# Fourier mixing over tokens split by mirror symmetry, in a two-layer diffusion block

## Chip and metric

The kernel runs on one core of a Trainium2 chip. The metric is the device time of one execution in microseconds, the median of several runs. The core has TensorE (PE in the rows, with PEld for its weight loads), VectorE (DVE), ScalarE (ACT), GpSimd (POOL) and SyncE (SP), which here issues most DMAs. DVE, ACT and POOL work on vectors; PE alone writes the accumulators in PSUM, in 8 banks of 512 fp32 columns.

## The reference

Two layers work on 512 latent tokens and 256 context tokens of 1024 channels; the last layer (layer 1) only on the latent ones. Each layer has a token mixer of three branches (attention, Fourier mixing, an RWKV scan), gated and merged, and then a convolutional feed-forward part. The Fourier branch takes 512 channels in 4 groups of 128 and transforms over channels of a group and over tokens, keeping the real part:

```python
def _fourier(pf):
    B, T, _ = pf.shape
    z = jnp.fft.fftn(pf.astype(jnp.float32).reshape(B, T, F_GROUPS, F_GROUP_W), axes=(1, 3), norm='ortho')
    return z.real.reshape(B, T, D_F).astype(pf.dtype)
...
    y = g[..., 0, :] * (o_a @ lp['w_pa']) + g[..., 1, :] * (o_f @ lp['w_pf']) + g[..., 2, :] * (o_c @ lp['w_pc'])
    return y @ lp['w_o']
```

## The kernel before

The kernel is written engine by engine, with semaphores. The function `close` is the last stage of a layer's token mixer; it runs once in layer 0 (768 tokens) and once in layer 1 (512). Its PE program is a list of 24 slots: 8 slots `pc` (one output tile of 128 channels each, product of the RWKV result with `w_pc`), 8 slots `pf` (Fourier result with `w_pf`), 8 slots `o` (output projection). A `pc` or `pf` slot has four contraction tiles k, and for each three products (high part by high weight, low part by high weight, high part by low weight), since every operand is split into two fp32r parts whose sum is nearly fp32. So a slot is 12 products, each of 512 and, in layer 0, 256 columns; `fm_product` (L370) issues them.

For each slot n, ACT applies the sigmoid to the slot's gate, then splits the weights of slot n + 2 (`split`, L2023: `w_hi`; it waits for the end of slot n, since the ring holds two), POOL computes `w_lo`, DVE multiplies the slot's result by the gate (L2124) and adds it to `y` (L2129). SP loads weights and gates ahead, in program order.

The Fourier transform is put between the products of the `pc` slots, one step after the second k (h = 0) and one after the fourth (h = 1) of a slot. For group j, a `z` step multiplies two token tiles of the input `f` by a 128 x 256 table of cosines and sines over channels (`dft_w`, L1938), and DVE copies the result into `z`, a double buffer (L2072). When all of a group's `z` is there, the `of` step sums over tokens with the full cosine and sine tables `dft_lat` (512 x 512 each, L1947) and `dft_ctx` (256 x 256 each, L1951). ACT rounds the result out of PSUM to `of_hi` (L2038), DVE takes the rest as `of_lo` (L2075). The first `pf` slot (slot 8) waits for `of_lo` of group k before its k-th contraction tile. All these transform matmuls are plain fp32. A list sets the order:

```python
dft = [s for j in range(F_GROUPS) for s in [("z", j, i) for i in range(HT2)] + [("of", j, 0)]]
dft_at = {(n, h): dft[2 * n + h] for n in range(KT) for h in range(2) if 2 * n + h < len(dft)}
```

The buffers `f` and `z` lie in the space of `x`, which is read back from memory behind the weights of slot 11.

Of the kernel before, what the change touches and what calls it, by code (L numbers as in the profile page):

```python
# [22 lines left out]
F32 = mybir.dt.float32  # L23
# [6 lines left out]
P = 128  # L30
# [40 lines left out]
def tables():  # L71
# [63 lines left out]
def program(nc, A, out):  # L135
    with ExitStack() as top:
# [1701 lines left out]
        def close(l, oc, y, rings, last):  # L1838
# [7 lines left out]
            dft = [s for j in range(F_GROUPS) for s in [("z", j, i) for i in range(HT2)] + [("of", j, 0)]]  # L1846
            dft_at = {(n, h): dft[2 * n + h] for n in range(KT) for h in range(2) if 2 * n + h < len(dft)}
# [8 lines left out]
            with ExitStack() as s2, stage(nc) as (block, sem):  # L1856
# [657 lines left out]
```

## Time and profile before

| | |
|---|---|
| median of 3 runs | 3658.41 us (3656.13 to 3660.78) |
| profiled execution, span from first to last instruction | 3653.4 us |
| median of the runs less that span | 5.0 us |
| PE busy | 3375.0 us, 92% of the span |
| DVE, ACT, POOL busy | 1582.8, 1268.5, 1071.4 us |
| closing stage of layer 0, slots 0 to 8 | about 1277.5 to 1362.9 us |
| closing stage of layer 1, slots 0 to 8 | about 3112.8 to 3179.4 us |

The profiled execution's own time beside its span isn't recorded; the runs' median lies 5.0 us above the span. Busy time is an average over stages; what a change is worth is read in the stage that it touches.

### The profile page before, as it was taken

To read this page: it belongs to the slowest core of one execution; us is meant where nothing else is said; L and a number is where in the kernel's file an instruction comes from. 1 tells how busy PE (TensorE), PEld (TensorE's weight loads), DVE (VectorE), ACT (ScalarE), POOL (GpSimd) and SP (SyncE) were. 2 spreads that over 40 slices of the span, in tenths; PEclk is the share of its full clock that TensorE was granted. 3 is DMA by queue.
4 is the path that set the end of the run, shared out by engine and by line. 5 is a ranking of instruction groups with operands and counts; after the bars stand their busy time and mean duration, and the time that the engine had idled before them with its cause. 6 is when DMAs were issued, how large, how long until landed. Compare 5 with 4: busy or idle time off the path is not lost. (4 is left out here: it accounts for less than half of the span.)

```text
span 3653.4 us, 82760 instructions
## 1 busy us (share of the span) xinstructions
PE 3375.0 (92%) x36725; PEld 2696.8 (74%) x36725; DVE 1582.8 (43%) x2538; ACT 1268.5 (35%) x2184; POOL 1071.4 (29%) x645
## 2 busy tenths in 40 slices
PE   6989999999888999799999899999899898889998
PEld 4668888888655777687878676887778666568887
DVE  3243334442377546512112734445453476372224
ACT  3333233333365412321212243334344465233222
POOL 1111133233011412332333132223333114235553
PEclk8999999999999999999999999999999999989999
DMA  7664333443212343233332145344343313423332
GB/s 260 213 204 113 111 113 90 119 121 96 83 58 96 102 140 104 81 116 121 116 116 94 50 142 182 101 113 128 115 128 92 104 58 121 165 84 104 98 98 87
DMA packets 444861, 423.43 MB, mean 116 GB/s; under 512 B 15652, under 2 KB 372042, under 8 KB 437594
## 3 DMA queue, kind: packets, MB, share of 16 engines
q1 hardware_dynamic: 442922, 409.35, 35.7%
q10 hardware_dynamic: 1584, 8.78, 0.6%
q8 instruction: 291, 4.77, 0.5%
q14 instruction: 64, 0.52, 0.0%
HBM read 329.34 MB, written 88.74 MB: 114 GB/s over the span
## 5 line engine op out<-in xcount | busy, mean ns | idle before, releaser
L893 PE MATMUL ps<-I-321_h_hi,I-324_w_hi 128*128 128x256 f32 (+1 forms) x832 | 294.8, 354 | 4.5 <-PEq L124 4.5
L893 PE MATMUL ps<-I-322_h_lo,I-324_w_hi 128*128 128x256 f32 (+1 forms) x832 | 282.0, 339 | 0.0
L893 PE MATMUL ps<-I-321_h_hi,I-325_w_lo 128*128 128x256 f32 (+1 forms) x832 | 281.8, 339 | 0.0
L2372 POOL TENSOR_TENSOR I-18800_w_lo<-I-18798_w_raw,I-18799_w_hi 128x1024 fp32r<-128x1024 f32 x60 | 145.1, 2418 | 342.6 <-ACT I-18799_w_hi L2335 342.5
L893 PE MATMUL ps<-I-23550_h_hi,I-23553_w_hi 128*128 128x512 f32 (+1 forms) x544 | 212.7, 391 | 4.6 <-PEq L124 4.6
L893 PE MATMUL ps<-I-23551_h_lo,I-23553_w_hi 128*128 128x512 f32 (+1 forms) x544 | 200.9, 369 | 0.0
L893 PE MATMUL ps<-I-23550_h_hi,I-23554_w_lo 128*128 128x512 f32 (+1 forms) x544 | 200.6, 369 | 0.0
L2372 POOL TENSOR_TENSOR I-39040_w_lo<-I-39038_w_raw,I-39039_w_hi 128x1024 fp32r<-128x1024 f32 x60 | 144.5, 2408 | 154.6 <-ACT I-39039_w_hi L2335 154.6
L2335 ACT ACTIVATE I-18799_w_hi<-I-18798_w_raw 128x1024 fp32r<-128x1024 f32 x61 | 64.6, 1059 | 355.0 <-PE ps L370 235.3
L370 PE MATMUL ps<-I-18795_h_hi,I-18799_w_hi 128*128 128x512 f32 x704 | 182.8, 341 | 1.1 <-DVE I-18796_h_lo L407 1.1
L370 PE MATMUL ps<-I-18795_h_hi,I-18800_w_lo 128*128 128x512 f32 x704 | 182.6, 340 | 0.0
L370 PE MATMUL ps<-I-18796_h_lo,I-18799_w_hi 128*128 128x512 f32 x704 | 180.1, 337 | 0.0
L893 PEld LDWEIGHTS ps<-I-321_h_hi,I-324_w_hi 128*128 128x128 f32 x832 | 158.5, 191 | 25.4 <-issue 4.9
L857 POOL TENSOR_TENSOR I-325_w_lo<-I-323_w_raw,I-324_w_hi 128x1024 fp32r<-128x1024 f32 x34 | 81.9, 2408 | 320.1 <-ACT I-324_w_hi L1137 320.1
L893 PEld LDWEIGHTS ps<-I-321_h_hi,I-325_w_lo 128*128 128x128 f32 x832 | 158.5, 191 | 17.2
L893 PEld LDWEIGHTS ps<-I-322_h_lo,I-324_w_hi 128*128 128x128 f32 x832 | 158.8, 191 | 14.6
L1119 ACT ACTIVATE I-1999_result<-ps 128x512 f32<-128x512 f32 x104 | 51.3, 493 | 327.7 <-PE ps L893 327.5
L857 POOL TENSOR_TENSOR I-23554_w_lo<-I-23552_w_raw,I-23553_w_hi 128x1024 fp32r<-128x1024 f32 x34 | 83.7, 2462 | 275.7 <-ACT I-23553_w_hi L1137 275.7
L963 PE MATMUL ps<-I-49_x 64*64 64x32 f32 x3840 | 149.3, 220 | 1.4 <-issue 1.4
L370 PE MATMUL ps<-I-39035_h_hi,I-39039_w_hi 128*128 128x512 f32 x352 | 137.9, 392 | 1.1 <-DVE I-39036_h_lo L407 1.1
L370 PE MATMUL ps<-I-39036_h_lo,I-39039_w_hi 128*128 128x512 f32 x352 | 137.1, 389 | 0.0
L370 PE MATMUL ps<-I-39035_h_hi,I-39040_w_lo 128*128 128x512 f32 x352 | 137.0, 389 | 0.0
(902 smaller groups left out, 8757.7 us busy)
## 6 DMA issues: line engine op xcount, KB each, us to landing
I-323_w_raw<-in_w_in SPq DMA_DIRECT2D x67, 512.0 KB, 5.8
I-23552_w_raw<-in_w_in SPq DMA_DIRECT2D x67, 512.0 KB, 5.2
I-18808_ada_w<-in_ada_w SPq DMA_DIRECT2D x24, 1024.0 KB, 6.0
I-18798_w_raw<-in_ffn_up SPq DMA_DIRECT2D x44, 512.0 KB, 3.8
I-39038_w_raw<-in_ffn_up SPq DMA_DIRECT2D x44, 512.0 KB, 3.8
proj_d<-I-1999_result SPq DMA_DIRECT2D x52, 384.0 KB, 3.0
I-507_ada_w<-in_ada_w SPq DMA_DIRECT2D x16, 1024.0 KB, 5.8
I-18798_w_raw<-in_ffn_down SPq DMA_DIRECT2D x22, 512.0 KB, 3.3
```

Of the source, the lines that this page charges most:

```text
L370: m = pe.matmul(dst[:, at:at + n], w[wi][:, k, :], a[ai][:, k, at:at + n], start=k == 0 and i == 0, stop=k == kt - 1 and i == 2)
L857: pool.tensor_tensor(lo(s), raw(s), hi(s).bitcast(F32), ALU.subtract).then_inc(sem("w_lo"), 1)
L893: m = pe.matmul(bank(6 + i % 2, n_c), w[:, k, :], hv[:, k, c0:c0 + n_c], start=k == 0 and v == 0, stop=k == KT - 1 and v == 2)
L963: return pe.matmul(side(ps[rows(i), (2 + d) * 512 + c0:(2 + d) * 512 + c0 + C], n_lv, 1 - d), Y[d][rows(i), c0:c0 + C], side(TT[d][rows(i) ...
L1119: act.activation(res[:, s % 2, c0:c0 + n_c], bank(6 + i % 2, n_c), ACT.Copy, scale=DH_A ** -0.5 if J_Q <= slots[s][0] < J_K else 1.0).then ...
L2335: act.activation(pair(g)[0], rings[0][:, g % 3, :, :], ACT.Copy).then_inc(sem("w_hi"), 1)
L2372: pool.tensor_tensor(pair(g)[1], rings[0][:, g % 3, :, :], pair(g)[0].bitcast(F32), ALU.subtract).then_inc(sem("w_lo"), 1)
```

## The change

The token transform is folded. For tokens t and n - t, cosine tables are equal and sine tables opposite, so the input's mirrored tokens are summed (DVE) and subtracted (POOL) once, for all groups: blocks E0, E1 (sums), O0, O1 (differences), E0M (a second form of the first block, which odd outputs need), and CE, CO, CEM for the context. A `z` step now multiplies 128-token blocks by the cosine or the sine table alone (128 columns each): 8 blocks a group in layer 0, 5 in layer 1, in two steps. The `of` step computes half of the outputs: even-numbered cosine outputs, odd-numbered cosine outputs (both written to every second column of PSUM) and sine outputs, from tables with half the rows. ACT copies the sine half out of PSUM (`odd`), DVE forms output m as cosine less sine and output n - m as cosine plus sine, in descending order, and copies outputs 0 and n/2; ACT then rounds to `of_hi` and DVE takes `of_lo`, both now from SBUF. The steps stand at other places: the first `z` after slot 1, the last `of` in the middle of slot 7, and each `of_hi`/`of_lo` half a slot after its sums.

```diff
-        both = np.stack([np.cos(at) * s, -np.sin(at) * s])
+        half = n // 2
+        folded = np.concatenate([np.cos(at)[:half, 0:half + 1:2], np.cos(at)[:half, 1:half:2], np.sin(at)[:half, 1:half]], 1) * s
...
-            dft = [s for j in range(F_GROUPS) for s in [("z", j, i) for i in range(HT2)] + [("of", j, 0)]]
-            dft_at = {(n, h): dft[2 * n + h] for n in range(KT) for h in range(2) if 2 * n + h < len(dft)}
+            dft = [("z", 0, 0), ("z", 0, 1)]
+            for j in range(F_GROUPS):
+                dft += [("z", j + 1, 0), ("of", j, 0), ("z", j + 1, 1)] if j + 1 < F_GROUPS else [("of", j, 0)]
+            dft_at = {((i + 3) // 2, (i + 3) % 2): s for i, s in enumerate(dft)}
+            rest_at = {((i + 4) // 2, (i + 4) % 2): j for i, (kind, j, _) in enumerate(dft) if kind == "of"}
+            E0, E1, O0, O1, E0M, CE, CO, CEM = range(8)
+            z_blocks = ((E0, E1, O0, O1), (E0M,) if last else (E0M, CE, CO, CEM))
...
-                    sp.dma_start(dw[:, :], A["dft_w"]).then_inc(sem("f"), 16)
                     gate_in(0)
                     weights(2)
-                    sp.dma_start(dl[:, :, :, :], A["dft_lat"]).then_inc(sem("dft"), 16)
-                    sp.dma_start(dc[:, :, :, :], A["dft_ctx"]).then_inc(sem("dft"), 16)
+                    sp.dma_start(dw[:, :], A["dft_w"]).then_inc(sem("dft"), 16)
+                    sp.dma_start(dl[:, :, :], A["dft_lat"]).then_inc(sem("dft"), 16)
+                    sp.dma_start(dc[:, :, :], A["dft_ctx"]).then_inc(sem("dft"), 16)
...
                             if c == 0:
-                                pe.wait_ge(sem("f"), 32)
+                                pe.wait_ge(sem("dft"), 48)
+                                pe.wait_ge(sem("fold_e"), len(f_seqs))
+                                pe.wait_ge(sem("fold_o"), len(f_seqs))
                             if c >= 2:
                                 pe.wait_ge(sem("z"), c - 1)
-                            for t in (2 * i, 2 * i + 1):
-                                m = pe.matmul(bank(4 + c % 2, 2 * P, (t % 2) * 2 * P), f[:, j, t * P:(t + 1) * P], dw[:, :], start=True, stop=True)
+                            for q, b in enumerate(z_blocks[i]):
+                                w = dw[:, P:2 * P] if b in (O0, O1, CO) else dw[:, 0:P]
+                                m = pe.matmul(bank(4 + i, P, q * P), fold[:, j, b, :], w, start=True, stop=True)
...
-                            pe.wait_ge(sem("z"), HT2 * (j + 1))
+                            pe.wait_ge(sem("z"), 2 * j + 2)
                             if j:
-                                pe.wait_ge(sem("of_lo"), j)
-                            for i in range(2 * LT):
-                                m = pe.matmul(bank(6), z[:, j % 2, i % LT, (i // LT) * P:(i // LT + 1) * P], dl[:, i // LT, i % LT, :],
-                                              start=i == 0, stop=i == 2 * LT - 1)
...
+                                pe.wait_ge(sem("of_sum"), j)
+                            for (_, n, e, o, em, at), table in zip(f_seqs, (dl, dc)):
+                                half, last_k = n // 2, n // (2 * P) - 1
+                                cos_e, cos_o, sin = slice(0, half // 2 + 1), slice(half // 2 + 1, half + 1), slice(half + 1, n)
+                                for k in range(last_k + 1):
+                                    pe.matmul(ps[:, at:at + half + 1:2], z[:, j % 2, e + k, :], table[:, k, cos_e], start=k == 0, stop=k == last_k)
+                                for k in range(last_k + 1):
+                                    pe.matmul(ps[:, at + 1:at + half + 1:2], z[:, j % 2, e + k if k else em, :], table[:, k, cos_o],
+                                              start=k == 0, stop=k == last_k)
+                                for k in range(last_k + 1):
+                                    m = pe.matmul(ps[:, at + half + 1:at + n], z[:, j % 2, o + k, :], table[:, k, sin], start=k == 0, stop=k == last_k)
...
                                 act.wait_ge(sem("ofmm"), j + 1)
-                                act.activation(ofp[0][:, j, :], of_ps, ACT.Copy).then_inc(sem("of_hi"), 1)
+                                if j >= 2:
+                                    act.wait_ge(sem("of_sum"), j - 1)
+                                for o, w, _, _, _, at in f_seqs:
+                                    m = act.activation(odd[:, j % 2, o // 2:o // 2 + w // 2 - 1], ps[:, at + w // 2 + 1:at + w], ACT.Copy)
+                                m.then_inc(sem("odd"), 1)
+                            if (n, h) in rest_at:
+                                j = rest_at[n, h]
+                                act.wait_ge(sem("of_sum"), j + 1)
+                                act.activation(ofp[0][:, j, :], of[:, j % 2, 0:n_tok], ACT.Copy).then_inc(sem("of_hi"), 1)
...
+                        pool.tensor_tensor(blocks_of(o, half // P)[:, :, 1:half], f[:, :, at + 1:at + half],
+                                           f[:, :, at + w - 1:at + half:-1], ALU.subtract).then_inc(sem("fold_o"), 1)
...
+                        for dst, n in ((blocks_of(e, half // P), half), (blocks_of(em, 1), P)):
+                            dve.tensor_tensor(dst[:, :, 1:n], f[:, :, at + 1:at + n], f[:, :, at + w - 1:at + w - n:-1], ALU.add)
...
+                                dve.tensor_tensor(v[:, 1:half], even[:, 1:half], sines, ALU.subtract)
+                                dve.tensor_tensor(v[:, w - 1:half:-1], even[:, 1:half], sines, ALU.add)
+                                m = dve.tensor_copy(v[:, 0:half + 1:half], even[:, 0:half + 1:half])
+                            m.then_inc(sem("of_sum"), 1)
...
+                    def of_rest(j):
+                        dve.wait_ge(sem("of_hi"), j + 1)
+                        dve.tensor_tensor(ofp[1][:, j, :], of[:, j % 2, 0:n_tok], ofp[0][:, j, :].bitcast(F32), ALU.subtract).then_inc(sem("of_lo"), 1)
```

The order on each engine follows from these lists, so it is shown at two places. First PE, layer 0, an `of` step among the products of a `pc` slot, in the kernel before (`ps` is PSUM, `I-49_x` the space of `x` in which `z` lies):

```order
L370 MATMUL ps<-I-17273_oc_hi,I-13892_w_lo 128x512
L370 MATMUL ps<-I-17273_oc_hi,I-13892_w_lo 128x256
L1947 MATMUL ps<-I-17276_dft_lat,I-49_x 128x512 x8
L1951 MATMUL ps<-I-17277_dft_ctx,I-49_x 128x256 x4
L370 MATMUL ps<-I-17273_oc_hi,I-13891_w_hi 128x512
```

The `of` step of group 0 after the change, in the middle of slot 3 of layer 0, on the same engine:

```order
L371 MATMUL ps<-I-17273_oc_hi,I-13892_w_lo 128x512
L371 MATMUL ps<-I-17273_oc_hi,I-13892_w_lo 128x256
L1961 MATMUL ps<-I-17276_dft_lat,I-49_x 128x129 x2
L1963 MATMUL ps<-I-17276_dft_lat,I-49_x 128x128 x2
L1966 MATMUL ps<-I-17276_dft_lat,I-49_x 128x255 x2
L1961 MATMUL ps<-I-17277_dft_ctx,I-49_x 128x65
L1963 MATMUL ps<-I-17277_dft_ctx,I-49_x 128x64
L1966 MATMUL ps<-I-17277_dft_ctx,I-49_x 128x127
L371 MATMUL ps<-I-17273_oc_hi,I-13891_w_hi 128x512
```

Twelve matmuls of 512 or 256 columns became nine of 64 to 255 columns. The second place is DVE in slots 6 and 7 of layer 0; before, from the copy of `z` in slot 6 to the last `of_lo`:

```order
L2072 COPY I-49_x<-ps 128x512
L2124 TENSOR_TENSOR I-17263_gated<-I-17262_gate,ps 128x768
L2129 TENSOR_TENSOR I-13889_y<-I-13889_y,I-17263_gated 128x768
L2072 COPY I-49_x<-ps 128x512 x2
L2124 TENSOR_TENSOR I-17263_gated<-I-17262_gate,ps 128x768
L2129 TENSOR_TENSOR I-13889_y<-I-13889_y,I-17263_gated 128x768
L2075 TENSOR_TENSOR I-17272_of_lo<-ps,I-17271_of_hi 128x768
```

On the same engine after the change, from the sums of group 2 in slot 6 to the first of group 3 in slot 7 (`I-49_x` now also holds `odd` and the sums):

```order
L2117 TENSOR_TENSOR I-49_x<-ps,I-49_x 128x255
L2118 TENSOR_TENSOR I-49_x<-ps,I-49_x 128x255
L2119 COPY I-49_x<-ps 128x2
L2117 TENSOR_TENSOR I-49_x<-ps,I-49_x 128x127
L2118 TENSOR_TENSOR I-49_x<-ps,I-49_x 128x127
L2119 COPY I-49_x<-ps 128x2
L2178 TENSOR_TENSOR I-17263_gated<-I-17262_gate,ps 128x768
L2183 TENSOR_TENSOR I-13889_y<-I-13889_y,I-17263_gated 128x768
L2124 TENSOR_TENSOR I-17272_of_lo<-I-49_x,I-17271_of_hi 128x768
L2109 COPY I-49_x<-ps 128x512
L2117 TENSOR_TENSOR I-49_x<-ps,I-49_x 128x255
```

The six sums came in ahead of the slot's gate product, and the copy of `z` that the `of` step of group 3 needs stands behind them and behind `of_lo`.

## Rows read from the trace of the kernel before

**Rows 1.** The page: span, then busy us, share and instructions of each engine.
```profile
span 3653.4 us, 82760 instructions
PE 3375.0 (92%) x36725; PEld 2696.8 (74%) x36725; DVE 1582.8 (43%) x2538; ACT 1268.5 (35%) x2184; POOL 1071.4 (29%) x645
```
**Rows 2.** Windows, layer 0: length, busy us of five engines (count), clock, DMA share, GB/s.
```profile
1320.00:1340.00 20.00, 20.00 (x89) 14.54 (x88) 8.60 (x8) 3.95 (x6) 2.56 (x2) 1.00 0.22 66
```
**Rows 3.** Timeline, DVE: start, length, line, output and inputs, [idle before, releaser].
```profile
1320.71 0.96 DVE L2075 TENSOR_TENSOR I-17272_of_lo<-ps,I-17271_of_hi 128x768 fp32r<-128x768 f32 x1 [6.59 <-ACT I-17271_of_hi L2038]
...
1340.30 0.96 DVE L2075 TENSOR_TENSOR I-17272_of_lo<-ps,I-17271_of_hi 128x768 fp32r<-128x768 f32 x1 [6.59 <-ACT I-17271_of_hi L2038]
...
3134.58 0.69 DVE L2075 TENSOR_TENSOR I-37914_of_lo<-ps,I-37913_of_hi 128x512 fp32r<-128x512 f32 x1 [10.86 <-ACT I-37913_of_hi L2038]
...
3160.51 0.69 DVE L2075 TENSOR_TENSOR I-37914_of_lo<-ps,I-37913_of_hi 128x512 fp32r<-128x512 f32 x1 [9.83 <-ACT I-37913_of_hi L2038]
```
**Rows 4.** Timeline, PE, an `of` step of layer 0.
```profile
1291.50 7.03 PE L1947 MATMUL ps<-I-17276_dft_lat,I-49_x 128*128 128x512 f32 x16
...
1298.37 1.89 PE L1951 MATMUL ps<-I-17277_dft_ctx,I-49_x 128*128 128x256 f32 x8
```
**Rows 5.** Timeline, PE, layer 0: the first and the last of 22 products.
```profile
1370.25 0.51 PE L370 MATMUL ps<-I-17271_of_hi,I-13892_w_lo 128*128 128x512 f32 x2
...
1377.61 0.51 PE L370 MATMUL ps<-I-17271_of_hi,I-13892_w_lo 128*128 128x512 f32 x2
```
**Rows 6.** Timeline, PE, attention of layer 0: 128-column fp32 products and their successors.
```profile
984.74 1.60 PE L1462 MATMUL ps<-I-13901_v_tm,I-13906_a_T 128*128 128x128 f32 x12
986.18 0.98 PE L1451 MATMUL ps<-I-50_ident,I-13902_E 128*128 128x128 f32 x6
```
**Rows 7.** Line 963 (the scan): passes' ns min/median/max, first and last start, shapes.
```profile
L963 PE MATMUL ps<-I-49_x x3840: 186/219/291, 296.4 to 2831.4; 64*64 64x32 f32 x192
```
**Rows 8.** Groups by line, ACT, both closing stages: count, busy us, mean ns, idle before.
```profile
L2023 ACT ACTIVATE I-13891_w_hi<-I-13890_w_raw 128x512 fp32r<-128x512 f32 x14 | 8.8, 628 | 37.7 <-PE ps L370 30.9 <-DMA I-13890_w_raw<-in_w_pf 5.8 <-DMA I-13890_w_raw<-in_w_pc 1.0
...
L2038 ACT ACTIVATE I-17271_of_hi<-ps 128x768 fp32r<-128x768 f32 x4 | 3.2, 812 | 30.0 <-PE ps L1951 30.0
...
L2038 ACT ACTIVATE I-37913_of_hi<-ps 128x512 fp32r<-128x512 f32 x4 | 2.4, 589 | 12.9 <-PE ps L1947 12.9
```
**Rows 9.** Groups by line, DVE, closing stage of layer 0.
```profile
L2124 DVE TENSOR_TENSOR I-17263_gated<-I-17262_gate,ps 128x768 f32<-128x768 f32 x15 | 14.3, 955 | 25.3 <-PE ps L370 18.8 <-issue 4.2 <-ACT I-17262_gate L2031 2.2
L2072 DVE COPY I-49_x<-ps 128x512 f32<-128x512 f32 x12 | 8.2, 687 | 8.5 <-PE ps L1938 8.5
```
**Rows 10.** Timeline, PE: two waits in later slots of both closing stages.
```profile
1380.83 0.61 PE L370 MATMUL ps<-I-17271_of_hi,I-13891_w_hi 128*128 128x512 f32 x2 [2.70 <-POOL I-13892_w_lo L2060]
...
3184.51 1.98 PE L2004 MATMUL ps<-I-37906_part,I-51_ones 128*128 128x512 f32 x4 [2.33 <-DVE I-37906_part L2139]
```
**Rows 11.** Windows after those two waits (the clock is the third figure from the end).
```profile
1381.00:1385.00 4.00, 4.00 (x15) 3.38 (x16) 3.97 (x7) 1.79 (x3) 1.28 (x1) 0.57 0.71 197
3185.00:3191.00 6.00, 6.00 (x25) 4.36 (x24) 3.00 (x6) 2.23 (x4) 0.00 (x0) 1.00 0.97 412
```
**Rows 12.** Timeline, PE: the waits at the start of both closing stages.
```profile
1282.50 1.13 PE L1938 MATMUL ps<-I-17275_dft_w,I-49_x 128*128 128x256 f32 x4 [0.80 <-DMA I-17275_dft_w<-in_dft_w]
...
3112.83 0.79 PE L370 MATMUL ps<-I-37915_oc_hi,I-35365_w_hi 128*128 128x512 f32 x1 [4.13 <-DVE I-37916_oc_lo L2116]
...
3117.03 2.08 PE L1938 MATMUL ps<-I-37917_dft_w,I-49_x 128*128 128x256 f32 x4 [1.27 <-DMA I-37917_dft_w<-in_dft_w]
...
3124.80 7.13 PE L1947 MATMUL ps<-I-37918_dft_lat,I-49_x 128*128 128x512 f32 x16 [0.56 <-DMA I-37919_dft_ctx<-in_dft_ctx]
```
**Rows 13.** Groups by line, POOL, closing stage of layer 0.
```profile
L2060 POOL TENSOR_TENSOR I-13892_w_lo<-I-13890_w_raw,I-13891_w_hi 128x512 fp32r<-128x512 f32 x14 | 18.1, 1292 | 101.8 <-ACT I-13891_w_hi L2023 101.8
```
**Rows 14.** Timeline, DVE, layer 1: gate products of slots 6 and 7.
```profile
3173.72 0.69 DVE L2124 TENSOR_TENSOR I-37905_gated<-I-37904_gate,ps 128x512 f32<-128x512 f32 x1 [1.46 <-PE ps L370]
...
3176.52 0.69 DVE L2124 TENSOR_TENSOR I-37905_gated<-I-37904_gate,ps 128x512 f32<-128x512 f32 x1 [1.38 <-PE ps L370]
```

More of the change, by code:

```diff
@@ L1949, in transform @@
-                            if not last:
-                                for i in range(2 * CT):
-                                    m = pe.matmul(bank(7, 256), z[:, j % 2, LT + i % CT, (i // CT) * P:(i // CT + 1) * P], dc[:, i // CT, i % CT, :],
-                                                  start=i == 0, stop=i == 2 * CT - 1)
+                                pe.wait_ge(sem("of_sum"), j)
[9 more added lines that the diff above has]
+                                    m = pe.matmul(ps[:, at + half + 1:at + n], z[:, j % 2, o + k, :], table[:, k, sin], start=k == 0, stop=k == last_k)
@@ L2057, in _ @@
                 def _(pool):
+                    for at, w, _, o, _, _ in f_seqs:
+                        pool.memset(blocks_of(o, w // (2 * P))[:, :, 0:1], 0.0)
+                    pool.wait_ge(sem("f"), 16)
+                    for at, w, _, o, _, _ in f_seqs:
+                        half = w // 2
+                        pool.tensor_tensor(blocks_of(o, half // P)[:, :, 1:half], f[:, :, at + 1:at + half],
+                                           f[:, :, at + w - 1:at + half:-1], ALU.subtract).then_inc(sem("fold_o"), 1)
                     for n in range(2, N):
@@ L2071, in transformed @@
                                 dve.wait_ge(sem("ofmm"), j - 1)
[L2072 removed]
+                            dve.tensor_copy(z[:, j % 2, 4 * i:4 * i + n, :].rearrange("p a b -> p (a b)"), bank(4 + i, n * P)).then_inc(sem("z"), 1)
                         else:
[L2074 to L2075 removed]
+                            dve.wait_ge(sem("odd"), j + 1)
+                            if j >= 2:
+                                dve.wait_ge(sem("of_lo"), j - 1)
+                            for o, w, _, _, _, at in f_seqs:
+                                half, v = w // 2, of[:, j % 2, o:o + w]
+                                even, sines = ps[:, at:at + half + 1], odd[:, j % 2, o // 2:o // 2 + half - 1]
+                                dve.tensor_tensor(v[:, 1:half], even[:, 1:half], sines, ALU.subtract)
[5 more added lines that the diff above has]
+                        dve.tensor_tensor(ofp[1][:, j, :], of[:, j % 2, 0:n_tok], ofp[0][:, j, :].bitcast(F32), ALU.subtract).then_inc(sem("of_lo"), 1)
                     def y_rest(j):
@@ L2116, in _ @@
                         dve.tensor_tensor(ocp[1][:, k, :], oc[:, k, 0:n_tok], ocp[0][:, k, :].bitcast(F32), ALU.subtract).then_inc(sem("oc_lo"), 1)
+                    dve.wait_ge(sem("f"), 16)
+                    for at, w, e, _, em, _ in f_seqs:
+                        folds(at, w, e, em)
                     for n in range(M):
+                        if (n, 0) in rest_at:
+                            of_rest(rest_at[n, 0])
                         if (n, 0) in dft_at:
@@ L2129, in _ @@
                         dve.tensor_tensor(yj, yj, pr[:, n % 2, 0:n_tok], ALU.add).then_inc(sem("ysum"), 1)
+                        if (n, 1) in rest_at:
+                            of_rest(rest_at[n, 1])
                         if (n, 1) in dft_at:
```

28 lines of the change are left out of this document (16 added, 12 removed).

## The prediction

> **What bounds the kernel now.** I read the page first: TensorE is busy for 92% of the span and no other engine for half of it [rows 1], so a change to TensorE's work counts at full size wherever TensorE runs without gaps. Next, the windows over the two closing stages, the only ones that the change touches: in layer 0, from 1320 to 1340 us, PE is busy in all 20 us at the full 2.4 GHz [rows 2]. Then the timeline there, engine by engine. DVE's `of_lo` of two neighbouring groups starts 19.57 us apart in layer 0; in layer 1 two groups take 25.93 us [rows 3]. DVE and ACT wait for PE in between. The stage is bound by PE alone, and its rhythm tells what the transform costs.
>
> **PE, removed.** Each fp32 matmul shows as two passes. The `of` step of layer 0 starts 16 latent passes at 1291.50 and the first context pass at 1298.37: 0.429 us for 512 columns, so 0.215 for 256 [rows 4]. A group is three `z` steps of 4 passes (2.58), 16 latent passes (6.87) and 8 context passes (1.72): 11.17 us. The rhythm agrees: 21 products after 1370.25 the clock stands at 1377.61, 0.350 us each [rows 5], so two slots of 12 take 8.40, and 19.57 less that is 11.17. In layer 1 a group is 1.72 and 6.87, 8.59 us; half of 25.93 less one and a half slots of 2.80, the distance of two slots without transform [rows 14], leaves 8.77, a little of it waiting.
>
> **PE, added.** The nearest row for 128 columns on fresh weights is the attention's fp32 product: 12 passes start at 984.74 and what follows them at 986.18, 0.120 a pass [rows 6]. Per group, layer 0: `z` is 8 blocks, 16 passes, 1.92; the latent part 8 passes of 128 or 129 columns at 0.120 and 4 of 255 at 0.214, 1.82; the context part 6 short passes, which I also take at 0.120, 0.72; together 4.46. Layer 1: 10 passes (1.20) and 1.82, 3.02. Saved: 4 x (11.17 - 4.46) = 26.8 and 4 x (8.59 - 3.02) = 22.3, **49.1 us**. If short passes cost only their columns (0.107 for 128), 3.3 us more is saved.
>
> Two thirds of the latent passes now write every second PSUM column, which the trace does not show. Bounds: the small products of the scan write runs with holes between them, and all 3840 of their passes lie between 186 and 291 ns, the median 219 [rows 7], which speaks for no cost; the bound above is that the latent ones take twice their columns' time, 0.214 in place of 0.120: 8 x 0.094 x 8 groups = 6.0 us. I take nothing, being nearest to rows 7, and keep 6.0 for the range.
> The Trainium skill speaks against the change here: its page "SBUF — State Buffer", section "Door 1: The DMA port swizzle", says that PSUM has lines of two fp32 values and that any non-contiguous access there slows matmuls significantly. No row of before writes single columns with gaps; by that rule, read as a doubling, the time would be the rival's below, by rows 7 it is the forecast's.
>
> **The waits that take part of it back.** Before, a result went PE, ACT (`of_hi`), DVE (`of_lo`), while PE had `z` steps of the next group ahead. Now it is a chain through four instructions, ACT (`odd`), DVE (sums), ACT (`of_hi`), DVE (`of_lo`), and three of its places in the program put it behind other work. In slots 3, 6 and 7 ACT must first split the weights of slot n + 2, and that waits for the END of slot n; `odd` stands behind it though its matmuls end mid-slot. DVE waits for `odd`, and behind that wait are the slot's gate product and addition, the `of_lo` and the copy of `z` that PE's next `of` needs. Prices: split 0.63 [rows 8]; `odd` 255 + 127 columns: the PSUM copy is 0.81 for 768 and 0.59 for 512 [rows 8], so 0.37 + 0.26, and 0.37 in layer 1; sums: DVE takes 0.955 for a product of 768 and 0.687 for a copy of 512 [rows 9], 1.05 ns a column on 0.15, so 2 x 0.42 + 2 x 0.28 + two tiny copies 0.3 = 1.65 (pipelined), and 1.0 in layer 1; gate product, addition, `of_lo` at a spacing of 0.90 and 0.62; the copy 0.68, or 0.28 for a single block; 0.1 for each change of engine.
>
> - From the end of slot 6, layer 0: 0.1 + 0.63 + 0.63 + 0.1 + 1.65 + 3 x 0.90 + 0.68 + 0.1 = 6.6 us until the `z` of group 3 is whole. PE has a `z` step (0.96) and half a slot (2.10) before `of` of group 3: a stall of 3.5. Layer 1: 4.5 against 0.24 + 1.40: 2.9.
> - From the end of slot 7: the same without the copy, 5.8, until `of_lo` of group 3; slot 8 needs it at its fourth k, 3.15 later: 2.6. Layer 1: 4.1 against 2.1: 2.0.
> - From the end of slot 3, group 0: 6.6 against 0.96 + 4.20 + 0.96: 0.5; layer 1: 4.5 against 0.24 + 2.80 + 0.96: 0.5.
> - In slot 5 DVE's `of_lo` of group 1 waits for ACT, again behind a split: 0.1 + 0.63 + 0.81 + 0.1 + 0.95 + 0.68 + 0.1 = 3.4 from the end of the slot, against 0.96 + 2.10: 0.4; layer 1 about the same, 0.4.
>
> Layer 0 loses 7.0, layer 1 5.8: **12.8 us**. If reversed operands take DVE twice as long, for which no row speaks (L2117 writes ascending, L2118 descending), each sum grows by 0.70 and 0.42, over 4 groups in each layer 4.5 us more.
>
> The clock: after a gap of 2.70 us before 1380.83 the granted clock was 0.57 of full on average from 1381 to 1385, half clock for most of them, which lost 4 x 0.43 = 1.7 us; after a gap of 2.33 before 3184.51 it stayed at 1.00 [rows 10, 11]. Of the stalls above two are longer than 2.70 and two are at or below it: 2 x 1.7 = **3.4 us**, with 0 and 6.8 as ends.
>
> **The start.** Layer 1 starts at 3112.83, waits 1.27 for `dft_w` and 0.56 for `dft_ctx`, and reaches its first `of` at 3124.80 [rows 12]: 11.97 us for 18 products and 2 `z` steps, which cost 5.9 at full clock: 6.1 lost, 1.8 of it in those waits, the rest to the clock after a wait of 4.13. Now 24 products run first without a wait, and I take half of the loss as gone; the tables shrink from 2.5 MB to 0.63, all landing before PE asks. Against that stand the folds: DVE 1020 and 508 columns (1.2 + 0.7 + two tiny, 2.2 us; 3.9 with the context), and POOL 1020 (+ 508) at 1292 ns for 512 [rows 13], 2.6 (+ 1.3), while each delays the other. They begin when `f` lands, just before 1282.50 and 3117.03, where `dft_w` behind it in the queue ends a wait [rows 12]. In layer 1 they end near 3120, where PE gets there; in layer 0 between 1286 and 1289.5, PE arriving near 1288. DVE's first gate product stands behind the folds, but slot 2 alone asks for it; POOL's split for slot 2 likewise. I take 3 us gained in layer 1 and 1 lost in layer 0, **2 us** gained, ends -2 and +4.
>
> **Nothing else moves.** Slots without transform ran 2.80 us apart in layer 1 (3173.72 to 3176.52) [rows 14], 12 products of 0.233, so loading weights and gates hides behind products alone. `x` returns on SP behind the gate of slot 11, which waits for slot 8's gate product, later than `of_lo`; the stall that it brings after [rows 10] stays.
>
> **The sum.** 49.1 + 2 - 12.8 - 3.4 = 34.9 us. The profiled execution spans 3653.4 us, so 3618.5 after; the median of the runs lies 5.0 above that span, and I keep that distance: **3623.5 us**.
>
> **Rivals.**
> - Strided PSUM writes slow the matmuls: + 6 us and up, 3630 to 3640. For it: no row writes single columns. Against it: rows 7. Chance 0.14.
> - The waits don't bind, since ACT or DVE runs ahead of my walk: 12.8 and 3.4 come back, 3607. Against it: `odd` stands behind the split in every one of the three slots. Chance 0.10.
> - More waiting than walked (clock falls in four places, folds late, reversed operands twice as long): 3.4 + 4 + 4.5 more, 3635 to 3640. Chance 0.10.
> - Slower than before: reversed operands run element by element on DVE. A sum's reversed half is 0.70 us in layer 0 and 0.42 in layer 1, and each of the 8 sums lies on a chain without slack; 34.9/(4 x 1.12) = 7.8, so from some nine times the plain duration on the time exceeds 3658. No row of DVE speaks for such a factor. Chance 0.05.
> - My forecast, all of it within 3613 to 3634: 0.61.
>
> The range 3610 to 3639 leaves out most of the second rival, the slow one and the edges. A measurement of this kernel tells 0.2% (7 us) from no change: faster 0.93, same 0.02, slower 0.05.
>
> **What would show it.** Right: `z` passes near 0.12 us apart; PE idle near 3 us in slot 7 before the `of` of group 3, released by DVE's copy, and near 2.5 us in slot 8, released by `of_lo`; `odd` on ACT always after a split; time from the first product of the stage to the end of slot 8 shorter by about 16 to 20 us in each layer. Wrong: cosine passes of 128 columns spaced over 0.2 us, sums over 2 us on DVE, or PE waiting for the folds by more than 2 us.

## The result and the profile after

The changed kernel takes 3616.11 us in the median of four runs (3612.46 to 3627.61) against 3657.27 before: a ratio of 0.9896, 95% interval 0.9881 to 0.9911. Its profiled execution took 3612.46 us and spans 3610.6, 42.8 less than the span in [rows 1]. The page (busy us, share and instructions of each engine):

```profile
span 3610.6 us, 82796 instructions
PE 3321.2 (92%) x36709; PEld 2677.0 (74%) x36709; DVE 1601.1 (44%) x2582; ACT 1271.8 (35%) x2196; POOL 1081.1 (30%) x651
```

PE lost 54 us of work, DVE and POOL gained 18 and 10. To see where the time went I cut the span at the first product of each closing stage and at DVE's gate product of slot 8, which ends the part that the change touches:

| us | start to layer 0 | stage, layer 0 | between | stage, layer 1 | to the end |
|---|---|---|---|---|---|
| before | 1277.49 | 85.73 | 1749.61 | 66.60 | 473.97 |
| after | 1274.55 | 66.50 | 1749.05 | 46.36 | 474.14 |

The two stages became 19.2 and 20.2 us shorter, 39.5 together (forecast 34.9); the other 3.3 lie where nothing was changed. The timeline of PE in layer 0 shows the price of the transform, and what it gives back (start, busy us, tile, passes, [idle before, releaser]):

```profile
1274.55 1.01 PE L371 MATMUL ps<-I-17273_oc_hi,I-13891_w_hi 128*128 128x512 f32 x2 [4.62 <-DVE I-17274_oc_lo L2165]
...
1288.05 1.13 PE L1951 MATMUL ps<-I-17275_dft_w,I-17278_folded 128*128 128x128 f32 x8 [2.24 <-issue]
...
1291.12 1.06 PE L1951 MATMUL ps<-I-17275_dft_w,I-17278_folded 128*128 128x128 f32 x8
...
1294.12 1.05 PE L1951 MATMUL ps<-I-17275_dft_w,I-17278_folded 128*128 128x128 f32 x8
...
1297.12 0.61 PE L1961 MATMUL ps<-I-17276_dft_lat,I-49_x 128*128 128x129 f32 x4
1297.57 0.61 PE L1963 MATMUL ps<-I-17276_dft_lat,I-49_x 128*128 128x128 f32 x4
1298.01 1.03 PE L1966 MATMUL ps<-I-17276_dft_lat,I-49_x 128*128 128x255 f32 x4
...
1301.63 1.06 PE L1951 MATMUL ps<-I-17275_dft_w,I-17278_folded 128*128 128x128 f32 x8
...
1319.01 0.71 PE L1961 MATMUL ps<-I-17276_dft_lat,I-49_x 128*128 128x129 f32 x4 [0.58 <-DVE I-49_x L2109]
...
1329.66 0.71 PE L1961 MATMUL ps<-I-17276_dft_lat,I-49_x 128*128 128x129 f32 x4 [2.85 <-DVE I-49_x L2109]
...
1339.71 0.62 PE L371 MATMUL ps<-I-17271_of_hi,I-13891_w_hi 128*128 128x512 f32 x2 [2.09 <-DVE I-17272_of_lo L2124]
```

Two `z` steps start 3.00 us apart with six products (2.10) between them: 0.90 for 8 passes, 0.112 a pass. Four strided cosine passes take 0.45 and 0.44, the same 0.112; an `of` step is 4.51 - 2.10 = 2.41. A group costs 2 x 0.90 + 2.41 = 4.21 us (11.17 before). In layer 1 a slot's half is six products of 0.233, 1.40:

```profile
3103.22 1.05 PE L1951 MATMUL ps<-I-37963_dft_w,I-37966_folded 128*128 128x128 f32 x8
...
3105.50 0.61 PE L1961 MATMUL ps<-I-37964_dft_lat,I-49_x 128*128 128x129 f32 x4
...
3108.64 0.38 PE L1951 MATMUL ps<-I-37963_dft_w,I-37966_folded 128*128 128x128 f32 x2
...
3110.26 1.06 PE L1951 MATMUL ps<-I-37963_dft_w,I-37966_folded 128*128 128x128 f32 x8
```

The distances 2.28, 3.14 and 1.62 less 1.40 are `z` steps of 0.88 and 0.22 and an `of` of 1.74, which make 2.84 a group (8.59 before). There PE stands three times for long enough to be listed:

```profile
3120.77 0.71 PE L1961 MATMUL ps<-I-37964_dft_lat,I-49_x 128*128 128x129 f32 x4 [0.63 <-DVE I-49_x L2109]
...
3128.22 0.71 PE L1961 MATMUL ps<-I-37964_dft_lat,I-49_x 128*128 128x129 f32 x4 [2.40 <-DVE I-49_x L2109]
...
3135.46 0.50 PE L371 MATMUL ps<-I-37959_of_hi,I-35411_w_hi 128*128 128x512 f32 x1 [1.73 <-DVE I-37960_of_lo L2124]
```

Why PE waits before 1329.66 is read on ACT and DVE, from the end of slot 6 (1323.9) on. ACT first:

```profile
1323.91 0.63 ACT L2037 ACTIVATE I-13891_w_hi<-I-13890_w_raw 128x512 fp32r<-128x512 f32 x1 [6.27 <-PE ps L371]
1324.44 0.54 ACT L2055 ACTIVATE I-49_x<-ps 128x255 f32<-128x255 f32 x2
1326.32 0.84 ACT L2060 ACTIVATE I-17271_of_hi<-I-49_x 128x768 fp32r<-128x768 f32 x1 [1.34 <-DVE I-49_x L2119]
```

and DVE:

```profile
1325.01 0.42 DVE L2117 TENSOR_TENSOR I-49_x<-ps,I-49_x 128x255 f32<-128x255 f32 x1 [3.60 <-ACT I-49_x L2055]
1325.35 0.41 DVE L2118 TENSOR_TENSOR I-49_x<-ps,I-49_x 128x255 f32<-128x255 f32 x1
...
1326.20 0.94 DVE L2178 TENSOR_TENSOR I-17263_gated<-I-17262_gate,ps 128x768 f32<-128x768 f32 x1
1327.18 0.96 DVE L2183 TENSOR_TENSOR I-13889_y<-I-13889_y,I-17263_gated 128x768 f32<-128x768 f32 x1
1328.06 0.95 DVE L2124 TENSOR_TENSOR I-17272_of_lo<-I-49_x,I-17271_of_hi 128x768 fp32r<-128x768 f32 x1
1328.93 0.68 DVE L2109 COPY I-49_x<-ps 128x512 f32<-128x512 f32 x1
```

ACT waited 6.27 us for PE to end slot 6, though the `of` step had ended at 1321.5: `odd` (L2055) stood behind the split (L2037). Then every link follows on the one before, and the copy (L2109) that PE needs comes last. The reversed sum (L2118) takes 0.41, the ascending one 0.42.

### The profile page after: what moved, and what is told of

Its sections match the earlier page's. It is cut to its first block and busy times, and to the rows that moved or that the text cites. A ratio compares the mean times of both kernels' runs of the same rounds, so it can differ in the third digit from the quotient of the medians.

```text
span 3610.6 us, 82796 instructions
## 1 busy us (share of the span) xinstructions
PE 3321.2 (92%) x36709; PEld 2677.0 (74%) x36709; DVE 1601.1 (44%) x2582; ACT 1271.8 (35%) x2196; POOL 1081.1 (30%) x651
## 5 line engine op out<-in xcount | busy, mean ns | idle before, releaser
L2428 POOL TENSOR_TENSOR I-18846_w_lo<-I-18844_w_raw,I-18845_w_hi 128x1024 fp32r<-128x1024 f32 x60 | 145.1, 2418 | 342.7 <-ACT I-18845_w_hi L2391 342.6
L894 PE MATMUL ps<-I-23596_h_hi,I-23599_w_hi 128*128 128x512 f32 (+1 forms) x544 | 211.6, 389 | 4.7 <-PEq L125 4.7
L894 PE MATMUL ps<-I-23597_h_lo,I-23599_w_hi 128*128 128x512 f32 (+1 forms) x544 | 199.9, 367 | 0.0
L894 PE MATMUL ps<-I-23596_h_hi,I-23600_w_lo 128*128 128x512 f32 (+1 forms) x544 | 199.6, 367 | 0.0
L2428 POOL TENSOR_TENSOR I-39124_w_lo<-I-39122_w_raw,I-39123_w_hi 128x1024 fp32r<-128x1024 f32 x60 | 144.5, 2408 | 154.6 <-ACT I-39123_w_hi L2391 154.6
L371 PE MATMUL ps<-I-18841_h_hi,I-18845_w_hi 128*128 128x512 f32 x704 | 183.0, 341 | 1.1 <-DVE I-18842_h_lo L408 1.1
L371 PE MATMUL ps<-I-18841_h_hi,I-18846_w_lo 128*128 128x512 f32 x704 | 182.3, 340 | 0.0
L371 PE MATMUL ps<-I-18842_h_lo,I-18845_w_hi 128*128 128x512 f32 x704 | 180.1, 337 | 0.0
L371 PE MATMUL ps<-I-39119_h_hi,I-39123_w_hi 128*128 128x512 f32 x352 | 137.8, 392 | 1.2 <-DVE I-39120_h_lo L408 1.2
L371 PE MATMUL ps<-I-39120_h_lo,I-39123_w_hi 128*128 128x512 f32 x352 | 137.0, 389 | 0.0
```

What stands on the lines that cost most here:

```text
L371: m = pe.matmul(dst[:, at:at + n], w[wi][:, k, :], a[ai][:, k, at:at + n], start=k == 0 and i == 0, stop=k == kt - 1 and i == 2)
L894: m = pe.matmul(bank(6 + i % 2, n_c), w[:, k, :], hv[:, k, c0:c0 + n_c], start=k == 0 and v == 0, stop=k == KT - 1 and v == 2)
L2428: pool.tensor_tensor(pair(g)[1], rings[0][:, g % 3, :, :], pair(g)[0].bitcast(F32), ALU.subtract).then_inc(sem("w_lo"), 1)
```

## Experiments

The theory: PE's passes make the saving; a part is given back because `odd` stands behind the split, and `z` and `of_lo` behind the slot's gate product, and because the folds of DVE and POOL delay each other. Its rivals are with each run. The outside of the two stages, the same code in all, took 3497.7 to 3513.9 us in the profiled executions, 3497.7 and 3508.1 in two of the very same kernel, so the ratio of one kernel to before is blurred by some 5 us; each ratio is to runs of before that stand beside it. What an edit did is read from the two stages, cut as above. "Clock" counts how often the granted clock fell from 2.4 to 1.2 GHz in them after a wait of PE, the wait ahead of the first `z` step included; "standing" is the sum of PE's listed waits behind that step, in us.

| kernel | layer 0 | layer 1 | sum | clock | standing | ratio to before, 95% |
|---|---|---|---|---|---|---|
| before | 85.73 | 66.60 | 152.33 | | | |
| after | 66.50 | 46.36 | 112.86 | 0 | 10.28 | 0.9896 (0.9881 to 0.9911) |
| after again | 68.21 | 47.96 | 116.17 | 2 | 10.30 | 0.9904 (0.9890 to 0.9917) |
| `odd` first | 64.24 | 43.77 | 108.01 | 1 | 4.98 | 0.9890 (0.9876 to 0.9903) |
| folds on DVE | 65.44 | 45.43 | 110.87 | 1 | 10.29 | 0.9898 (0.9882 to 0.9913) |
| both | 60.08 | 42.77 | 102.85 | 0 | 4.97 | 0.9867 (0.9854 to 0.9881) |
| side by side | 68.18 | 47.67 | 115.85 | 2 | 10.29 | 0.9904 (0.9890 to 0.9919) |
| `z` twice | 73.35 | 49.12 | 122.47 | 1 | 7.98 | 0.9908 (0.9891 to 0.9924) |
| `z` copy first | 65.35 | 44.09 | 109.44 | 1 | 5.53 | 0.9887 (0.9872 to 0.9902) |
| all four edits | 57.46 | 39.65 | 97.11 | 0 | none | 0.9848 (0.9834 to 0.9863) |

**The changed kernel again.** 

> The changed kernel again, unaltered, so that the other kernels of this call have it beside them on the same chip. Every theory expects what its first runs showed: a ratio to the kernel before of 0.990 (0.989 to 0.991), 3616 us, and the same stalls of TensorE: in layer 0 2.24 us for the folds, 2.85 in slot 7, 2.09 in slot 8; in layer 1 2.40 and 1.73.

The waits in slots 7 and 8 came again to within 0.01. The wait ahead of the first `z` step did not: 2.67 us in layer 0 (2.24) and 1.70 in layer 1 (0.54), as more of the products ahead of it ran at the higher clock; the step itself began at the same place, 13.52 and 9.10 us after the first product (13.50 and 9.13). The median was 3623.86 us, 7.7 above that of the first four runs, and both stages were longer. PE on the stall in slot 7 and on the next row with a wait, then the clock after each (the third figure from the end), first of this run:

```profile
1333.48 0.71 PE L1961 MATMUL ps<-I-17276_dft_lat,I-49_x 128*128 128x129 f32 x4 [2.86 <-DVE I-49_x L2109]
...
1345.18 0.62 PE L371 MATMUL ps<-I-17271_of_hi,I-13891_w_hi 128*128 128x512 f32 x2 [2.09 <-DVE I-17272_of_lo L2124]
```
```profile
1335.00:1337.00 2.00, 2.00 (x8) 1.71 (x7) 0.00 (x0) 0.00 (x0) 0.00 (x0) 0.50 0.00 0
1337.00:1339.00 2.00, 2.00 (x12) 1.83 (x12) 0.00 (x0) 0.00 (x0) 0.00 (x0) 0.81 0.00 0
```

and of the first execution of the same kernel:

```profile
1329.00:1331.00 2.00, 1.34 (x10) 1.31 (x11) 0.61 (x2) 0.00 (x0) 0.00 (x0) 1.00 0.73 233
1331.00:1333.00 2.00, 2.00 (x15) 1.84 (x14) 0.00 (x0) 0.00 (x0) 0.00 (x0) 1.00 0.00 0
```

After 2.85 us of idling the clock stayed at 2.4 GHz in one execution; after 2.86 it fell to 1.2 GHz in the other, and the stretch from one row to the next took 11.70 in place of 10.05 us: 1.65 lost. The same happened in layer 1 (2.40 kept, 2.41 lost, again 1.65). Less these two falls the stages take 112.87 us, the 112.86 of the first execution: all of the difference inside them is the clock. Further on a fall is taken off in the same way, each with its own stretch, where two sums are compared.

**`odd` before the split.**

```diff
-                        if n + 2 < N:
-                            split(n + 2)
                         for h in range(2):
+                            if h and n + 2 < N:
+                                split(n + 2)
```

> ScalarE takes a group's `odd` (and `of_hi`) before the split of the weights of slot n + 2 wherever the group's matmuls end in mid-slot. Theory (the stalls come from `odd` standing behind a split that waits for the end of the slot): the chain starts up to half a slot (2.1 us in layer 0, 1.4 in layer 1) plus a split (0.5) earlier; the stalls before the `of` of group 3 and in slot 8, now 2.85 + 2.09 in layer 0 and 2.40 + 1.73 in layer 1, together 9.1, fall to between 1 and 4; the kernel is 5 to 8 us faster than the changed one, a ratio near 0.988. Rival (VectorE's longer work alone makes the stalls): they stay above 7 us together and the time moves by less than 2 us.

The waits in slots 7 and 8 fell from 9.07 to 4.98, those before group 2 went away. The clock fell once, after the wait for the folds (2.95 in this execution):

```profile
1295.03 1.23 PE L1951 MATMUL ps<-I-17275_dft_w,I-17278_folded 128*128 128x128 f32 x8 [2.95 <-issue]
...
1299.65 1.06 PE L1951 MATMUL ps<-I-17275_dft_w,I-17278_folded 128*128 128x128 f32 x8
```

From the first `z` step to the second it took 4.62 us, against 3.07 in the changed kernel (1288.05 to 1291.12 above): that fall cost 1.55. Without it 106.5: 6.4 us saved, inside the forecast, so the rival (DVE's work alone) falls. That 4.98 remain, not 1 to 4, has a cause of its own, which DVE and then POOL show in layer 0:

```profile
1332.36 1.89 DVE L2183 TENSOR_TENSOR I-13889_y<-I-13889_y,I-17263_gated 128x768 f32<-128x768 f32 x1
```
```profile
1332.14 1.30 POOL L2089 TENSOR_TENSOR I-13892_w_lo<-I-13890_w_raw,I-13891_w_hi 128x512 fp32r<-128x512 f32 x1 [6.20 <-ACT I-13891_w_hi L2037]
```

and in layer 1, in the same order:

```profile
3134.78 0.69 DVE L2183 TENSOR_TENSOR I-35409_y<-I-35409_y,I-37951_gated 128x512 f32<-128x512 f32 x1
3135.39 1.75 DVE L2124 TENSOR_TENSOR I-37960_of_lo<-I-49_x,I-37959_of_hi 128x512 fp32r<-128x512 f32 x1
```
```profile
3134.83 1.77 POOL L2089 TENSOR_TENSOR I-35412_w_lo<-I-35410_w_raw,I-35411_w_hi 128x512 fp32r<-128x512 f32 x1 [3.63 <-ACT I-35411_w_hi L2037]
```

DVE's addition, 0.96 us above, now takes 1.89, and the `of_lo` of layer 1, 0.68 in the changed kernel, 1.75: with `odd` gone first, POOL's work on the weights runs beside them, and no longer beside the sums. Ahead of each of the four waits that are left one such instruction is longer, by 0.9 in layer 0 and 1.1 in layer 1, 4.0 us together of the 4.98.

**All folds on DVE.**

```diff
-                    pool.wait_ge(sem("f"), 16)
-                    for at, w, _, o, _, _ in f_seqs:
-                        half = w // 2
-                        pool.tensor_tensor(blocks_of(o, half // P)[:, :, 1:half], f[:, :, at + 1:at + half],
-                                           f[:, :, at + w - 1:at + half:-1], ALU.subtract).then_inc(sem("fold_o"), 1)
...
+                        dve.tensor_tensor(blocks_of(o, half // P)[:, :, 1:half], f[:, :, at + 1:at + half],
+                                          f[:, :, at + w - 1:at + half:-1], ALU.subtract).then_inc(sem("fold_o"), 1)
```

> GpSimd's two subtracting folds and its memsets are given to VectorE, which then does all folds; GpSimd has nothing to do until its first split. Theory (folds on VectorE and GpSimd delay each other): VectorE's folds run at their own rate, 1.22 + 0.68 + 1.08 for f's latent part, 0.7 + 0.3 + 0.7 for the context part and some 0.6 for the single columns, about 5.5 us in layer 0 against 8.8 now; the wait of 2.24 us at the start of layer 0 falls under 0.5; 1.5 to 3 us faster than the changed kernel. Rival (VectorE is slow by itself, GpSimd's share costs it nothing): the folds then end 1.9 us later in layer 0 and 1.1 in layer 1, and the kernel is 2 to 3 us slower than the changed one.

In the changed kernel, DVE's two first folds, the single columns behind them, and the last fold:

```profile
1279.18 4.01 DVE L2097 TENSOR_TENSOR I-17278_folded<-I-49_x 128x1020 f32<-128x1020 f32 x2 [2.08 <-DMA I-49_x<-proj_d]
1283.11 1.23 DVE L2098 TENSOR_TENSOR I-17278_folded<-I-49_x 128x4 f32<-128x4 f32 x1
...
1286.72 1.24 DVE L2099 TENSOR_TENSOR I-17278_folded<-I-49_x 128x4 f32<-128x4 f32 x1
```

beside POOL's

```profile
1279.23 5.09 POOL L2085 TENSOR_TENSOR I-17278_folded<-I-49_x 128x1020 f32<-128x1020 f32 x2 [6.44 <-DMA I-49_x<-proj_d]
```

and with POOL idle, in this experiment:

```profile
1282.35 1.82 DVE L2090 TENSOR_TENSOR I-17278_folded<-I-49_x 128x1020 f32<-128x1020 f32 x2 [1.92 <-DMA I-49_x<-proj_d]
1284.08 0.16 DVE L2091 TENSOR_TENSOR I-17278_folded<-I-49_x 128x4 f32<-128x4 f32 x1
```

The two folds of 1020 and 508 columns take 1.82 in place of 4.01, four columns 0.16 in place of 1.23. In the changed kernel the profile puts PE's 2.24 us ahead of the first `z` step down to issue, but the last fold ended at 1287.96 and PE started at 1288.05. With the folds on DVE alone the wait is gone: the first `z` step starts 10.79 us after the first product (13.50 in the changed kernel) in layer 0 and 8.30 (9.13) in layer 1, 3.5 us together. One clock fall (1.65, after the 2.85 in slot 7) hides half of it in the sum; without it 109.2, 3.6 us shorter, more than the 1.5 to 3 that were expected. The theory holds, the rival (2 to 3 us slower) falls.

**Both.** The two diffs together. 

> The two edits together: `odd` before the split, and all folds on VectorE. If both theories hold the savings add, being in different stretches of the stage: 7 to 11 us faster than the changed kernel, about 3607, a ratio near 0.987. If both rivals hold it is as slow as the folds alone, 3618.

102.85, 10.0 us shorter, and the edits gave 6.4 and 3.6 apart: they add up. The ratio is 0.9867, below those of each alone. No wait here is longer than 1.75 us, and the clock never fell.

**Cosine outputs side by side.**

```diff
-                                    pe.matmul(ps[:, at:at + half + 1:2], z[:, j % 2, e + k, :], table[:, k, cos_e], start=k == 0, stop=k == last_k)
+                                    pe.matmul(ps[:, at:at + half // 2 + 1], z[:, j % 2, e + k, :], table[:, k, cos_e], start=k == 0, stop=k == last_k)
...
-                                    pe.matmul(ps[:, at + 1:at + half + 1:2], z[:, j % 2, e + k if k else em, :], table[:, k, cos_o],
+                                    pe.matmul(ps[:, at + half // 2 + 1:at + half + 1], z[:, j % 2, e + k if k else em, :], table[:, k, cos_o],
```

> The cosine passes write their columns side by side in place of every second column; VectorE then reads places that hold other outputs, so the result is scrambled and only the time counts. Theory (strided PSUM columns cost nothing): four passes of 128 or 129 columns stay 0.45 us apart, the two stages stay as long as in the changed kernel with the same gaps, within 1 us. Rival (every second column slows the matmul): the spacing falls and the stages get 3 to 6 us shorter.

```profile
1301.04 0.61 PE L1961 MATMUL ps<-I-17276_dft_lat,I-49_x 128*128 128x129 f32 x4
1301.48 0.61 PE L1963 MATMUL ps<-I-17276_dft_lat,I-49_x 128*128 128x128 f32 x4
1301.93 1.03 PE L1966 MATMUL ps<-I-17276_dft_lat,I-49_x 128*128 128x255 f32 x4
```

0.44 and 0.45 us for four passes, as with every second column. The clock fell twice, behind 2.85 and 2.40 of idling, and the stretches to PE's next wait took 11.67 us (10.05 in the changed kernel) and 8.65 (7.24): 3.03 lost, and 115.85 less that is 112.8, against 112.9. Strided fp32 writes cost nothing here. The Trainium skill, "SBUF — State Buffer", section "Door 1: The DMA port swizzle", has any non-contiguous access to PSUM slow matmuls significantly; for these writes the trace does not agree.

**Every `z` matmul twice.**

```diff
-                            for q, b in enumerate(z_blocks[i]):
+                            for q, b in [qb for qb in enumerate(z_blocks[i]) for _ in range(2)]:
```

> Every `z` matmul is issued twice, with the same output: 64 passes more in layer 0 and 40 in layer 1, at 0.112 us 7.2 + 4.5 = 11.7 us of TensorE's work. Theory (TensorE's passes are the price, except where the step lies in the half slot ahead of a stall): the second step of group 3 is absorbed by the stall in slot 7 (0.9 and 0.2), the one ahead of group 2's stall by 0.6 and 0.2; the stages get 9.5 to 11 us longer than in the changed kernel. Rival (the chain over ScalarE and VectorE sets the pace of the stages, and TensorE has room): less than 4 us.

```profile
1295.38 3.54 PE L1951 MATMUL ps<-I-17275_dft_w,I-17278_folded 128*128 128x128 f32 x16 [3.25 <-issue]
...
1300.97 1.95 PE L1951 MATMUL ps<-I-17275_dft_w,I-17278_folded 128*128 128x128 f32 x16
...
1304.83 1.95 PE L1951 MATMUL ps<-I-17275_dft_w,I-17278_folded 128*128 128x128 f32 x16
```

The stages take 122.47 us, 9.6 more, but 1.7 of it is the clock, which fell after 3.25 us of waiting for the folds: the second `z` step starts 5.59 us after the first, the third 3.86 after the second (3.07 and 3.00 in the changed kernel). So the stages are 8.0 us longer for 11.4 of added work (0.88 a step of four blocks, 0.21 for the single block of layer 1). The rest was absorbed where PE had waited in the changed kernel: by the distances between the steps, 0.9 and 0.2 us before group 3, 0.9 and 0.9 before group 2, 0.1 and 0.4 before group 1. TensorE sets the pace outside of the stalls; the rival (under 4) falls, and the size (9.5 to 11) was forecast too high, since the waits before groups 1 and 2 absorbed more than the 0.8 that were taken for them.

**`z` copied first.**

```diff
+                        if (n, 1) in dft_at and dft_at[n, 1][0] == "z" and n > 2:
+                            transformed(dft_at[n, 1])
                         dve.wait_ge(sem("w_used"), n + 1)
...
-                        if (n, 1) in dft_at:
+                        if (n, 1) in dft_at and not (dft_at[n, 1][0] == "z" and n > 2):
```

> From slot 3 on VectorE copies a finished `z` before the slot's gate product and addition instead of behind them; `odd` stays behind the split. Theory (the stall before group 3 is the whole chain, and the gate product and addition are 1.85 and 1.25 us of it): 2.85 falls to about 1.0 in layer 0 and 2.40 to 1.15 in layer 1, the 0.6 before group 2 go, those of slot 8 (2.09 and 1.73) stay: the stages get 4 to 5 us shorter than in the changed kernel. Rival (ScalarE's late `odd` alone decides when the copy can start): they stay within 1 us of it.

109.44, and 107.9 without a clock fall behind the wait for the folds (2.88; 1.55, worked out as for `odd` first): 5.0 us, the upper end of the forecast, but differently made up. In slot 7 of layer 0 no listed wait is left (forecast 1.0), since the copy also passed `of_lo`, 0.95, which I had overlooked; in layer 1 0.48 remains (forecast 1.15). The 0.6 before group 2 stayed: that copy stands in the first half of slot 5, behind `of_lo`, which this edit leaves. Slot 8 stayed at 2.10 and 1.73. So `odd` behind the split and the copy behind the gate product are two halves of one chain; shortening either gives the wait back.

**All four edits.** `odd` before the split, all folds on DVE and `z` copied first, and as a fourth DVE takes `of_lo` ahead of the slot's gate product and ACT `of_hi` ahead of the split.

```diff
                         for h in range(2):
                             kind, j, _ = dft_at.get((n, h), ("", 0, 0))
+                            if h and kind == "of" and n + 2 < N:
+                                split(n + 2)
...
+                        if dft_at.get((n, 1), ("",))[0] != "of" and n + 2 < N:
+                            split(n + 2)
...
+                        if (n, 1) in rest_at:
+                            of_rest(rest_at[n, 1])
                         dve.wait_ge(sem("w_used"), n + 1)
```

> All orders mended: folds on VectorE; ScalarE takes `odd` and `of_hi` before the split of slot n + 2 (except where the matmuls end with the slot); VectorE copies `z` and takes `of_lo` before the slot's gate product. Theory: of the stalls that are left with the first two edits (1.44 + 0.68 and 1.75 + 1.10) less than 1.5 us remains in both layers together; the two stages take about 99 us against 102.9 with the first two edits and 112.9 to 116.2 in the changed kernel; 3605, a ratio near 0.9855. Rival (the gate product that is moved back delays TensorE or y in turn): no shorter than with the first two edits, or a new wait of TensorE for `gated` or `y_lo` of over 2 us.

PE no longer waits from the first `z` step of a stage to slot 8 (windows; PE's busy time is the first figure behind the length, the clock the third from the end):

```profile
1284.00:1304.00 20.00, 20.00 (x136) 18.28 (x135) 13.71 (x21) 5.47 (x10) 5.01 (x3) 1.00 0.39 108
1304.00:1330.50 26.50, 26.50 (x174) 24.13 (x173) 17.77 (x32) 9.34 (x17) 5.43 (x4) 1.00 0.34 97
3093.00:3124.00 31.00, 31.00 (x173) 26.93 (x173) 19.96 (x39) 12.43 (x23) 9.96 (x7) 1.00 0.44 127
```

The stages take 97.11 us (about 99 forecast); the rival's new wait did not come. 3604.71 us in the median (3600.63 to 3608.20), a ratio of 0.9848 (0.9834 to 0.9863). Its interval touches neither of the changed kernel's (0.9881 to 0.9911 and 0.9890 to 0.9917), so this version beats both kernels; it also shows what the change is worth when no wait gives part of it back.

## Why the prediction held

3623.5 was forecast, 3616.11 measured, inside the range and on the forecast's side. The 7.4 us between them are no more than what the same kernel's two medians lie apart (3616.11 and 3623.86). Term by term, in the profiled execution:

- **Passes removed and added: 49.1 forecast, 50.8 measured**, 4 x (11.17 - 4.21) + 4 x (8.59 - 2.84). Passes of 128 columns went 0.112 apart, between the 0.120 taken from [rows 6] and the 0.107 of their columns alone. Strided writes: nothing, as taken, shown by the runs with and without gaps.
- **Waits: -12.8 forecast, -11.6 measured** by starts (the start after each wait less the start that the spacing before it would give; the idle listed is some 0.15 shorter each, since ends are modelled). Layer 0: 3.0 and 2.3 in slots 7 and 8 (forecast 3.5 and 2.6), 0.7 before group 2 (0.4), nothing before group 1 (0.5). Layer 1: 2.6 and 1.9 (2.9 and 2.0), 0.8 and 0.3 (0.4 and 0.5). Place, releaser and order were as walked; `odd` at 0.54, not 0.63, and sums of 1.3, not 1.65, made them shorter. That the order makes them is shown by the `odd` first, `z` copy first and all four edits runs. Those runs also give the size in another way: from the changed kernel to all four edits the stages lost 15.75 us, 3.29 of it ahead of the first `z` steps, which leaves 12.5 for the waits and the slower first step behind each.
- **The clock: -3.4 forecast, 0 in this execution**, -3.3 in another of the same kernel. The size of a fall was right (1.65 for 1.7); that idling beyond 2.70 brings one and less does not was wrong both ways (2.85 kept the clock here, 2.41 lost it there). That none came in the execution that is compared is chance.
- **The start: +2 forecast, +0.5 measured.** Layer 1 lost 3.5 in place of 6.1 (+2.6 for +3). Layer 0 lost 5.1 in place of 3.0 (-2.1 for -1): PE waited 2.24 for the folds, which I had named as a sign of being wrong. The mis-sized part is the folds' contention: I costed DVE's at 3.9 with the context, added only that "each delays the other", and they took 8.8, until 1287.96; on DVE alone they and POOL's share took 6.1.

50.8 - 11.6 + 0.5 = 39.7 against the 39.5 of the table. With nothing given back and the folds early the stages gain 152.33 - 97.11 = 55.2, which is 50.8 and 3.8 of better starts (the first `z` step 10.94 and 8.40 us after the first product, 0.5 and 3.3 less loss than before). The 0.6 that is left is about what the groups of layer 1 stood over their passes before (8.77 and 8.59 in the prediction, four groups, 0.7); with it and the 12.5 the sum above is 39.5 as well.

Of the rivals, slow strided writes and slow reversed operands are refuted (0.112 a pass, 0.41 for 0.42 a sum). "The waits don't bind" would have given 3607; they bound, at 11.6. Of "more waiting than walked" only the late folds came. The distance to the profiled execution, 3623.5 - 3612.46 = 11.0, is 4.6 inside the stages (3.4 of it the clock falls that did not come), 3.3 outside, which no edit explains, and 3.1 from the 5.0 that I put between span and median (1.9 in this run). So the mechanism held term by term, and the closeness of the total owes something to chance in the clock and outside the stages.

## What to carry to other kernels

When matmuls are replaced by elementwise steps, walk the new chain through each engine's program order: here 50.8 us of passes went and 11.6 came back because links of the chain stood behind work that waited for the end of a slot, and moving a few lines got them back. Before handing half of an elementwise step to GpSimd, read what VectorE's half costs beside it; doing all of it on VectorE ended 2.6 us earlier in layer 0. And compare stages, not spans, when an edit is worth less than the scatter of the rest of the program.

## What the hardware showed that was not expected

- The clock does not follow the length of a gap alone. At 2.85 or 2.86 us of idling before slot 7's `of` it stayed once and fell three times (after again, folds on DVE, side by side); at 2.40 or 2.41 it stayed twice and fell twice; at 2.20 and below no fall was seen in these slots. Of the waits for the folds in layer 0, those of 2.24 to 2.67 kept it and those of 2.88 to 3.25 lost it. A fall cost 1.4 to 1.7 us. What decides between equal gaps stays open.
- VectorE and GpSimd slow each other by operand: an addition of two SBUF tiles went from 0.96 to 1.89 us beside GpSimd's subtraction, two folds from 1.82 to 4.01, four columns from 0.16 to 1.23, while the sums with one operand in PSUM took 0.41 to 0.42 with GpSimd busy (its subtraction of 1.30 us at 1324.61 lies over those shown at 1325.01) as with GpSimd idle (`odd` first). The Trainium skill, "SBUF — State Buffer", section "Who interferes with whom", says that a VectorE instruction with two SBUF inputs contends with GpSimd's reads and that one with at most one, outside its two-port modes, does not; these rows agree.
- Which of the two is slowed goes by which began first. In the rows of `odd` first the addition that began at 3134.78, 0.05 us ahead of GpSimd's subtraction, kept its 0.69 and the subtraction took 1.77 for 1.30; the `of_lo` that began 0.56 behind that subtraction took 1.75 for 0.68, and the addition of layer 0 that began 0.22 behind GpSimd's took 1.89 for 0.96. In the other pairs with the weights' subtraction in slots 0 to 8 of these two kernels, the changed one and `odd` first, VectorE's instruction is likewise longer where it began second and not where it began first.
